# Halving the tokens at four stage boundaries of a fused transformer block

## The reference, cut to what matters

```
for i in range(2):
    h = rmsnorm(x, norm_g[i, 0]) * (1 + scale) + shift
    y = mixer(h)                       # a_in, a_out or m_in, m_out
    x = x + gate * rmsnorm(y, norm_g[i, 1])
    h = rmsnorm(x, norm_g[i, 2]) * (1 + scale) + shift
    y = swiglu_ffn(h)                  # f_in, f_out
    x = x + gate * rmsnorm(y, norm_g[i, 3])
# then: h = rmsnorm(x, norm_mix); h @ w_in; attention ...
```

## Time and profile before

| | us |
|---|---|
| median of three runs | 2296.62 (2295.95 to 2297.3) |
| profiled execution | 2297.04 |
| its span | 2295.2 |
| TensorE busy | 2223.1 (97%) |
| VectorE busy | 1242.6 (54%) |
| ScalarE busy | 994.1 (43%) |
| GpSimd busy | 974.2 (42%) |
| mean granted TensorE clock | 0.978 of full |

### The profile page before, as it was taken

One profiled execution on the slowest core, in us unless ns is written; L12 is line 12 of the kernel. 1 busy time (PEld: TensorE's weight loads), 2 busy tenths in 40 slices (PEclk: granted clock), 3 DMA queues, 4 the chain that ended last, 5 costly groups with the idle time before them and its releaser, 6 DMA issues.

```text
span 2295.2 us, 28959 instructions
## 1 busy us (share of the span) xinstructions
PE 2223.1 (97%) x10434; PEld 1761.0 (77%) x10434; DVE 1242.6 (54%) x1718; ACT 994.1 (43%) x1420; POOL 974.2 (42%) x421
## 2 busy tenths in 40 slices
PE   6999999999979999989999999999999899999998
PEld 4788888788867777767788888878677688888886
DVE  5876666521297787786522221250777755666412
ACT  4324443333435546554534334453555634444332
POOL 3544443446534333334444446556211143444563
PEclk8999899999989999999899999999999999999999
DMA  7553475553315344332133223334321032333232
GB/s 304 212 202 125 152 265 201 185 143 95 115 40 186 111 142 149 113 111 90 59 103 97 91 72 95 109 106 145 97 67 47 29 107 76 108 93 91 76 91 72
DMA packets 74096, 273.83 MB, mean 119 GB/s; under 512 B 8519, under 2 KB 11207, under 8 KB 67736
## 3 DMA queue, kind: packets, MB, share of 16 engines
q1 hardware_dynamic: 70632, 266.74, 35.6%
q10 hardware_dynamic: 3376, 5.90, 0.8%
HBM read 269.21 MB, written 8.12 MB: 121 GB/s over the span
## 4 chain that ended last, share of the span: by engine, by line
PE 76%; issue 14%; POOL 5%; DVE 3%; ACT 1%; DMA 0%; ACTq 0%; POOLq 0%; SPq 0%; DVEq 0%
PE bank L543 60%; POOL wlo L504 5%; PE bank L913 4%; PE bank L566 2%; PE bank L1006 2%; PE bank L970 1%; PE bank L934 1%; PE bank L953 1%; PE bank L570 1%; PE bank L607 1%; PE bank L615 1%; PE bank L654 1%; PE bank L854 0%; DVE x L1553 0%; DMA ada_first<-ada_d 0%
## 5 line engine op out<-in xcount | busy, mean ns | idle before, releaser
L504 POOL TENSOR_TENSOR wlo<-raw,whi 128x1024 fp32r<-128x1024 f32 x382 | 928.8, 2438 | 1235.9 <-ACT whi L1044 1235.7
L1044 ACT ACTIVATE whi<-raw 128x1024 fp32r<-128x1024 f32 x382 | 401.3, 1055 | 622.9 <-PE bank L543 588.3
L543 PE MATMUL bank<-h_hi,whi 128*128 128x512 f32 x1616 | 649.3, 402 | 4.9 <-DVE dt_tok L1878 2.5
L543 PE MATMUL bank<-h_hi,wlo 128*128 128x512 f32 x1616 | 638.1, 395 | 0.0
L543 PE MATMUL bank<-h_lo,whi 128*128 128x512 f32 x1616 | 636.0, 394 | 0.0
L543 PEld LDWEIGHTS bank<-h_hi,whi 128*128 128x128 f32 x1616 | 303.9, 188 | 79.6 <-issue 5.7
L543 PEld LDWEIGHTS bank<-h_hi,wlo 128*128 128x128 f32 x1616 | 303.8, 188 | 77.2
L543 PEld LDWEIGHTS bank<-h_lo,whi 128*128 128x128 f32 x1616 | 304.0, 188 | 70.4
L543 PE MATMUL bank<-g_hi,whi 128*128 128x512 f32 x592 | 236.3, 399 | 0.0
L543 PE MATMUL bank<-g_hi,wlo 128*128 128x512 f32 x592 | 233.2, 394 | 0.0
L543 PE MATMUL bank<-g_lo,whi 128*128 128x512 f32 x592 | 232.1, 392 | 0.0
(11 more groups left out here) (337 smaller groups left out, 2953.5 us busy)
## 6 DMA issues: line engine op xcount, KB each, us to landing
raw<-f_in_d SPq DMA_DIRECT2D x88, 512.0 KB, 3.5
raw<-m_d SPq DMA_DIRECT2D x65, 512.0 KB, 3.7
ada_f<-ada_d SPq DMA_DIRECT2D x24, 1024.0 KB, 7.0
raw<-g_in_d SPq DMA_DIRECT2D x44, 512.0 KB, 3.5
raw<-w_in_d SPq DMA_DIRECT2D x41, 512.0 KB, 3.6
csb<-cs_d SPq DMA_DIRECT2D x32, 640.0 KB, 6.5
ada_a<-ada_d SPq DMA_DIRECT2D x16, 1024.0 KB, 4.9
raw<-a_in_d SPq DMA_DIRECT2D x24, 512.0 KB, 6.0
```

The source lines that it names most:

```text
L504: nc.gpsimd.tensor_tensor(wlo[:, s], raw[:, s], whi[:, s].bitcast(F32), ALU.subtract).then_inc(lo_ready, 1)
L543: mm = nc.tensor.matmul(psum[bank][:], w[:, s, kk, :], xs[part == "lo"][:, k, :], start=first and kk == 0 and i == 0, stop=last and kk == ...
L1044: nc.scalar.activation(whi[:, s], raw[:, s], ACT.Copy).then_inc(hi_ready, 1)
```

## The change

The last `HALVED` tiles of the four stages (3, 1, 2 and 1 of them) are made by halves of the tokens: all first halves (columns 0 to 255), then all second halves. The pieces of y that ScalarE and VectorE work on are the full tiles, then the half ones. Sums, roots, spreads and norm of the first half run while TensorE is at the second halves; TensorE's sums and spreads stand at fixed places among its products (after 8, 20, 34 and 50 of them). The `four` chunks are done by halves too: first half of the tokens for chunks 0 and 1, chunk 2 joining at k = 3, chunk 3 after k = 7; then the second half, chunk 0 first. In the first half VectorE writes all the low parts, in the second half GpSimd does. The splits of the next stage's four chunks move behind the matmuls of the second halves, since the ring holds the chunks of the halved tiles until then; on ScalarE they stand between the pieces, the roots and the norm tiles, the last one behind norm tile 4 of the first half. The second halves' sums and roots stand inside `tiles(0)` on VectorE, after tiles 2, 5 and 6.

The loop over two groups of four f_out tiles becomes 7 tiles written out. The root's table is asked for at piece 4 instead of 5.

```diff
+HALVED = (3, 1, 2, 1)
+HALF = (slice(0, S // 2), slice(S // 2, S))
+def pieces(r):
+    full = KD - HALVED[r]
+    return [(m, None) for m in range(full)] + [(m, h) for h in range(2) for m in range(full, KD)]
...
+            def low_half(phase):
+                pool.wait_ge(in_ready, I0[phase] + KD)
+                for k in range(KD):
+                    pool.wait_ge(in_hi, I0[phase] + KD + k + 1)
+                    nc.gpsimd.tensor_tensor(h_lo[:, k, HALF[1]], tb[:, k % 2, HALF[1]], h_hi[:, k, HALF[1]].bitcast(F32),
+                                            ALU.subtract).then_inc(in_ready, 1)
...
+            def four(name, r):
...
+                opened(0)
+                opened(1)
+                for k in range(KD):
+                    if k == 3:
+                        opened(2)
+                        for kk in range(3):
+                            high(2, kk, 0)
+                            lower(2, kk, 0)
+                    turn(k, 0, (0, 1) if k < 3 else (0, 1, 2))
+                    if k == 3:
+                        sum_y(r, 1)
+                    elif k == 4:
+                        sum_xz(r, 1)
+                    elif k == 6:
+                        spread(Y_BANK[1], roots(r, 1, 0), R1, 1)
+                spread(Z_BANK[1], roots(r, 1, 1), R2, 1)
+                opened(3)
+                for k in range(KD):
+                    high(3, k, 0)
+                    lower(3, k, 0)
+                for k in range(4):
+                    turn(k, 1, range(4))
+                for k in range(4, KD):
+                    turn(k, 1, (0,))
+                for i in range(1, 4):
+                    for k in range(4, KD):
+                        high(i, k, 1)
+                        lower(i, k, 1)
+            def halves(name, r, cuts, xs):
...
+                products(0, 0, n * total)
+                products(1, 0, 8)
+                sum_y(r, 0)
+                products(1, 8, 20)
+                sum_xz(r, 0)
+                products(1, 20, 34)
+                spread(Y_BANK[0], roots(r, 0, 0), R1, 0)
+                products(1, 34, 50)
+                spread(Z_BANK[0], roots(r, 0, 1), R2, 0)
+                products(1, 50, n * total)
...
+            def norm_halves(r, name, y, sums, last_split):
+                norm_tile(r, 0, 0)
+                done(C0[name] + CHUNKS[name] - 1)
+                y_out(name, r, last_piece(r, 1), y, sums)
+                for k in range(1, 5):
+                    norm_tile(r, 0, k)
+                split_hi(last_split)
+                root_y(r, 1)
+                for k in range(5, KD):
+                    norm_tile(r, 0, k)
+                root_x(r, 1)
+                for k in range(KD):
+                    norm_tile(r, 1, k)
...
             def ffn(n):
-                for m in range(KD):
-                    y_tile(f_out, 1 + 2 * n, m, 4)
-                residual_roots(1 + 2 * n)
+                r = 1 + 2 * n
+                for m in range(KD - HALVED[r]):
+                    y_tile(f_out, r, m, 4)
+                first_halves(f_out, r, y, sums)
+                c = C0[f_out] + 4 * (KD - 1)
+                split_hi(c + RING)
+                root_x(r, 0)
+                split_hi(c + RING + 1)
+                split_hi(c + RING + 2)
+                if n == 0:
+                    act.wait_ge(ncol_ready, 7)
+                norm_halves(r, f_out, y, sums, c + RING + 3)
...
+            first_halves("a_out", 0, y, sums)
+            c = C0["a_out"] + KD - HALVED[0]
+            split_hi(c + RING)
+            y_out("a_out", 0, KD, y, sums)
+            root_x(0, 0)
+            split_hi(c + RING + 1)
+            y_out("a_out", 0, KD + 1, y, sums)
...
+            first_halves("m_out", 2, y_m, sums_m)
+            c = C0["m_out"] + 2 * (KD - HALVED[2])
+            split_hi(c + RING)
+            split_hi(c + RING + 1)
+            y_out("m_out", 2, KD, y_m, sums_m)
+            root_x(2, 0)
+            split_hi(c + RING + 2)
+            done(C0["m_out"] + CHUNKS["m_out"] - 1)
+            norm_halves(2, "m_out", y_m, sums_m, c + RING + 3)
...
+            def residual(r, name, phase, y, sums):
...
+                    for k in range(KD):
+                        w = added(k, v)
+                        if k == 0:
+                            dve.wait_ge(rb_done, roots(r, h, 1) + 1)
+                        elif k < KD - 1:
+                            v = grown(k + 1)
+                        step.wait(w)
+                        if k >= 2:
+                            dve.wait_ge(in_hi, I0[phase] + KD * h + k - 1)
+                        TT(ta[:, k % 2, cols], x[:, k, cols], psum[Z_BANK[h]][:, cols], ALU.mult).then_inc(t_out, 1)
+                        if k == 0:
+                            v = grown(1)
+                        elif h == 0:
+                            low(k - 1)
+                        if h == 0 and k == 2:
+                            piece_sums(name, r, last_piece(r, 1), y, sums)
+                        elif h == 0 and k == 5:
+                            first_root(1)
+                        elif h == 0 and k == 6:
+                            new_square(1)
+                    if h == 0:
+                        low(KD - 1)
+                for i in range(last_piece(r, 0) + 1):
+                    piece_sums(name, r, i, y, sums)
+                first_root(0)
+                new_square(0)
+                for i in range(last_piece(r, 0) + 1, last_piece(r, 1)):
+                    piece_sums(name, r, i, y, sums)
+                inverse(roots(r, 0, 1), R2, half(0))
+                tiles(0)
+                inverse(roots(r, 1, 1), R2, half(1))
+                tiles(1)
```

More of the change, by code:

```diff
@@ L88, with columns_of, last_piece, buffer_user @@
 I0, _ = starts(INS)
-BY_TILE = ("a_in", "f_in0", "m_in", "f_in1", "w_in")
+HALVED = (3, 1, 2, 1)
[3 more added lines that the diff above has]
+    return [(m, None) for m in range(full)] + [(m, h) for h in range(2) for m in range(full, KD)]
+def columns_of(h):
+    return slice(0, S) if h is None else HALF[h]
+def last_piece(r, h):
+    return KD - 1 + h * HALVED[r]
+PIECE0 = [sum(len(pieces(q)) for q in range(r)) for r in range(4)]
+ADDED0 = [sum(len(pieces(q)) - 1 for q in range(r)) for r in range(4)]
+def buffer_user(r, i):
+    ps = pieces(r)
+    users = [j for j in range(1, i) if j % 2 == i % 2 and (ps[j][1] is None or ps[j][1] == ps[i][1])]
+    return users[-1] if users else None
 VCOLS = dict(c=8, ada_b=96, norm_g=64, a_conv=24, m_conv=128, m_conv_b=32, m_norm=16, m_d=16,
@@ L520, in low @@
                                             ALU.subtract).then_inc(in_ready, 1)
-            first = 0
-            for phase in BY_TILE:
+            def low_half(phase):
[4 more added lines that the diff above has]
+                                            ALU.subtract).then_inc(in_ready, 1)
+            first = C0["a_in"] + RING
+            splits(0, first)
+            low("a_in")
+            for phase in ("f_in0", "m_in", "f_in1", "w_in"):
                 splits(first, C0[phase] + RING)
-                low(phase)
+                low_half(phase)
                 first = C0[phase] + RING
@@ L598, in down @@
+            def down(name, it, xs, tiles=4, first=0):
+                for m in range(first, first + tiles):
                     b = bank_of(T0[name] + m, it, 4)
@@ L691, in _ @@
                     modulation(10)
-            residual_roots(0, sums)
+            halves("a_out", 0, (8,), (g_hi, g_lo))
             def ffn(n):
                 if n == 0:
-                    four("f_in0", 1)
+                    four("f_in0", 0)
                     modulation(11)
```

308 lines of the change are left out of this document (171 added, 137 removed).

## The result

The changed kernel is slower: 2326.26 us median (2323.32 to 2328.40, 4 runs) against 2296.96 (2295.95 to 2298.91, 4 runs), ratio 1.0126 with a 95% interval of 1.0108 to 1.0143, which is +29 us (25 to 33). The forecast was +21.9.

A forecast was written before the change was run, and what follows sets the result against it. TensorE, busy 97%, was taken as the bound before, VectorE's chain in the changed joints. Joint costs 7.5 + 3.9 + 7.6 + 2.9 = +21.9 on the profiled 2297.04 gave 2318.9, median 2318.5 us; own range 2312 to 2325, wider 2298 to 2334.

The forecast's parts named there:

- rival (c): Slower still by the clock, which drops in gaps at J0 and J2: +27 to +45, 2324 to 2342; chance 0.17.
- The gap goes, VectorE's chain replaces it: At J3 the 10.7 us gap without products goes; VectorE's first half takes 18.2 us and TensorE waits for it.
- J3: Joint from f_out1 to w_in: stretch of 51.45 us forecast to end at 54.4, 2.9 later.
- Half product 0.117: Each of the 1368 half products on TensorE takes 0.117 us; upper bound 0.125.
- J1: Joint from f_out0 to m_in: stretch of 50.48 us forecast to end at 54.4, cost 3.9 through chunk 0.
- J0: Joint from a_out to f_in0, three halved tiles: stretch forecast at 61.3 us against 53.77, cost 7.5.
- J2: Joint from m_out to f_in1, two halved tiles: stretch forecast at 66.8 us against 59.25, cost 7.6.
- The norm behind the products: At J2 ScalarE takes up the norm only when all products are done, 31.2 us from the stretch's start.
- Locks: VectorE operations with both inputs in SBUF wait for GpSimd's running one; J3's first half has two, 1.3 and 1.6 us.
- Rival (b): Locks bite little, because GpSimd's splits fall where VectorE reads PSUM: +2 over the joints, 2299; chance 0.07.
- Rival (a), the overlap works: TensorE's own work, 185.7 us against 214.95, sets the four joints: 2267; chance 0.13 together with half way, about 2287.
- Rival (d), the load is not hidden: Weight load not hidden behind 256 columns: 1368 halves cost 97 us more, +88 with the rest, 2385; chance 0.03.

The follow-up runs named there:

- e1: Changed kernel with the products y*R1 of the half tiles written to PSUM instead of SBUF, so the add of x reads one PSUM operand: 2312.1 us, ratio 1.0070.
- e2: Changed kernel with GpSimd's splits of the sixteen shared weight chunks done over 8 of 128 columns (output lacks those low parts): 2315.8 us, ratio 1.0077.
- e12: Changed kernel with one halved tile at every joint, and ScalarE's order at J0 and J2 as at J1: 2316.76 us, ratio 1.0083.
- e5: Kernel before, with f_out1's 528 products of 512 columns done as 1056 of 256 (its values come out wrong): 2300.7 us, ratio 1.0017.
- e7: Changed kernel with 40 products that nobody reads put into TensorE's stall at J0 and J2: 2322.49 us, ratio 1.0101.
- e3: Changed kernel with the first half's second root taken and inverted before the second half's piece sums at J0 and J2: 2317.72 us, ratio 1.0099.
- e9: Changed kernel with e1's and e3's edits, first-half low parts on GpSimd, small root operations reading PSUM, second root chain one tile earlier: 2294.77 us, ratio 0.9991.
- e13: e9 with only the order of several instructions changed on GpSimd, TensorE and ScalarE in the joints: 2302.28 us, ratio 1.0025.

## Why the prediction came out as it did

The direction and the main mechanism were right, and the size was near: +21.9 forecast, +26.3 profile to profile (25.2 of it in the joints), +29 in the medians. The measured 2326 lies within the stated 2298 to 2334, but above the 2312 to 2325 of the forecast's own range and at the low end of rival (c)'s, the clock. Two joints came out 0.5 us each below the forecast and two 2.1 and 2.3 above it.

- *The gap goes, VectorE's chain replaces it.* Right. J3 followed the schedule to some tenths: first scaled half tile 16.5 us from the start (forecast 17.2), products' end 18.1 (18.8), the last root inverted at 35.5 (35.4), next scaled at 37.0 (37.6), last at 46.9 (47.9), end 53.8 (54.4). VectorE's first half took 18.9 us from the first scaled half tile (18.2). Within these the terms offset each other in part: the held operations of the first half cost 4.3 us (1.0, 1.5 and 1.8 above their own times) and not 2.9, the waits for ScalarE 1.5 and not 1.8, the second half's tiles 9.9 and not 10.3. That some tenths are left is partly luck. e1 and e2 each shortened VectorE's chain and the kernel, and e12, which took TensorE's cover away, did not make it slower.
- *Half product 0.117.* Too low by 0.003 (e5), 4 us over the 1368 halves if all were on the path. Not all are: J1 and J3 came out shorter than forecast.
- *J1 +3.9, J3 +2.9.* Measured +3.4 and +2.4; the wait for cs is 79.2 us from the stretch's start, 75.9 before, +3.3.
- *J0 +7.5, J2 +7.6.* Measured +9.6 and +9.9. The term that was mis-sized is the clock, which the sum had at nothing. The stall was placed well (J0 16.5 to 22.2, forecast 17.0 to 22.1; J2's root 24.5, forecast 24.6), and so was the first scaled half tile (23.4 and 25.9, forecast 23.1 and 25.9). The clock fell in the stall, so that the products behind it ended late, which costs 0.8 and 1.1 us up to the last root (e7). It fell again behind the last scaled half tile, which costs 1.4 us at each joint, in this execution: in others of the same code that interval lies at other joints or at none. The two together are the excess over the forecast (2.0 and 2.3) or slightly more, so how near the sum came depends on the execution that was profiled. The range did allow for a lower clock, at 1.2 us per joint under the second half and at 3 to 7 if it lasted through all products. This is part of rival (c), added to the forecast and not in its place.
- *The norm behind the products.* Right: at J2 ScalarE was forecast to take up the norm at 31.2, when all products are done, and did at 32.8. With the root taken ahead of the sums (e3) 5.5 of J2's 9.9 us go, so more than half of that price is the order of the work and not its amount.
- *Locks.* Right, and the largest single term: with the adds out of it (e1) 13 us, with short weight splits (e2) 11. Rival (b) had priced them near zero; the forecast's sum has them at about 20 in all, and no run took out all of them alone.
- *Rival (a), the overlap works.* False for this change, and not reached by any run: its joints are to take 185.7 us, TensorE's own work, and e9's, the shortest, take 208.35. Even those need another placing of operands, of low parts and of roots, and then the kernel just meets the one before.
- *Rival (d), the load is not hidden.* False by e5, where 0.120 us was measured with a full-array load of 0.187 us beside each half product. The Trainium skill, "TensorE: Matmul & The Clock Gate", section "The mechanism" (Part 3), has a load overlap matmuls only in other row groups. By that rule a half would step at 0.21 us, an estimate from the page's rates, and this case does not agree with it. The same section also names a background weight buffer as a target for which a load is pulled ahead; no run here tells whether that is what happens.

On the lock, the Trainium skill's page "SBUF — State Buffer", section "SBUF: two separate sides", lets a VectorE operation with two SBUF inputs and a GpSimd operation that reads SBUF exclude each other. e1 agrees: adds of 410/424/1443 ns became 407/415/422 when one operand left SBUF.

What stays open: 1.1 us of the profiled difference lie outside the joints, and the medians differ by 3 us more than the profiled executions; one profile of each doesn't tell where.

## What to carry to other kernels

Before laying work over a gap, count what the covering engine's neighbours must do in it: here TensorE's 10.7 us of waiting became VectorE's 18.9 us in series. VectorE has as many operations per half as per whole tile, pays for each with more than half (0.335 against 0.30 us started apart), took over the low parts, and got GpSimd's weight splits beside it. If VectorE must run beside GpSimd, leave one operand of each of its operations in PSUM, but look first whether the held operation is on the path: worth 13 us in the changed kernel and nothing in the old one. Moving a step earlier on one queue moves all that stands behind it; e3 gained 6 us that way and e13 lost 7.5. Before you call a stall harmless, follow what waits for the work behind it: at J2 it was ScalarE's norm.

## What the runs showed of the hardware

- Splitting 512-column products into 256-column ones costs 3% of their time (0.120 us each, where half of 0.233 is 0.1165), with a full weight load beside each (e5).
- VectorE's two-input operations were held until GpSimd's running operation was over whenever both inputs lay in SBUF (2.45 us for one of 0.41, the row at 228.00), and not when one lay in PSUM (64 adds of e1 within 407 to 422 ns), even where the output goes to SBUF. Writing the product to PSUM cost nothing (0.42 us).
- With TensorE standing for 5.35 us at J0 the granted clock fell to 1.2 GHz, and the half products behind the stall started 0.21 us apart for 0.12. With 40 products that nobody reads in the stall they started 0.12 apart.
- One half-clock interval of 3.4 us behind the last scaled half tile made the rest of the joint 1.4 to 1.5 us longer (6.94 to 8.34 at J2, 6.94 to 8.43 at J3). In executions of the same code it fell at different joints, so single stretches compare only to about that.
